# Gated attention in a two-layer block: backward direction in backward token order, GpSimd copying queries, keys and finished blocks

## The reference, cut to what matters

```
bcum = cumsum(a, within the chunk)
inter = (q * exp(bcum)) @ s
decay[t, s] = exp(bcum[t] - bcum[s])        for s <= t, per key column
scores[t, s] = sum_k q[t, k] k[s, k] decay[t, s, k]
intra = scores @ v
s_new = s * exp(total) + (k * exp(total - bcum)).T @ v
```

## Time and profile before

| | us |
|---|---|
| median of 3 runs | 3181.17 (3180.76 to 3181.77) |
| the profiled execution | 3191.26 |
| its span, first to last instruction | 3189.5 |
| PE busy in the span | 2585.3 (81%) |
| DVE busy | 1668.5 (52%) |
| ACT busy | 913.6 (29%) |
| POOL busy | 848.5 (27%) |

### The profile page before, as it was taken

One profiled execution on the slowest core, in us unless ns is written; L12 is line 12 of the kernel. 1 busy time (PEld: TensorE's weight loads), 2 busy tenths in 40 slices (PEclk: granted clock), 3 DMA queues, 4 the chain that ended last, 5 costly groups with the idle time before them and its releaser, 6 DMA issues. The chain is left out here.

```text
span 3189.5 us, 47594 instructions
## 1 busy us (share of the span) xinstructions
PE 2585.3 (81%) x19846; PEld 2207.7 (69%) x19846; DVE 1668.5 (52%) x2456; ACT 913.6 (29%) x1438; POOL 848.5 (27%) x779
## 2 busy tenths in 40 slices
PE   4899999965788763555594899999679999998787
PEld 1577677755677752554473677878579999998665
DVE  2136887542346524787556546465555554554333
ACT  1114233311132223355311323232233334332211
POOL 0211111126466531555322211111012211121321
PEclk7899999987789876777797899999889999999898
DMA  6613545533324312010243223333332222210521
GB/s 255 214 51 93 160 134 161 161 125 81 84 78 120 101 42 74 17 42 25 86 140 90 80 99 113 103 109 106 123 112 69 92 74 87 74 54 1 205 99 60
DMA packets 290100, 318.04 MB, mean 100 GB/s; under 512 B 109663, under 2 KB 235046, under 8 KB 287198
## 3 DMA queue, kind: packets, MB, share of 16 engines
q1 hardware_dynamic: 288816, 311.62, 30.8%
q10 hardware_dynamic: 1070, 3.37, 0.3%
HBM read 202.30 MB, written 112.56 MB: 99 GB/s over the span
## 5 line engine op out<-in xcount | busy, mean ns | idle before, releaser
L2668 PE MATMUL PS<-Q,K 128*128 128x128 f32 x2560 | 296.0, 277 | 33.0 <-DMA K<-k_d 24.1
L2668 PEld LDWEIGHTS PS<-Q,K 128*128 128x128 f32 x2560 | 292.5, 194 | 35.5 <-issue 28.1
L2789 POOL TENSOR_TENSOR weights_lo<-weights,weights_hi 128x1664 fp32r<-128x1664 f32 x32 | 121.4, 3793 | 566.6 <-ACT weights_hi L2747 566.6
L2695 PE MATMUL PS<-V_hi,weights_hi 128*128 128x258 f32 x832 | 239.1, 287 | 5.3 <-DVE H L2898 2.7
L376 PE MATMUL PS<-hT_hi,w_in_hi 128*128 128x512 f32 (+1 forms) x640 | 239.7, 375 | 0.0
L377 PE MATMUL PS<-hT_lo,w_in_hi 128*128 128x512 f32 (+1 forms) x640 | 236.4, 369 | 0.0
L378 PE MATMUL PS<-hT_hi,w_in_lo 128*128 128x512 f32 (+1 forms) x640 | 236.2, 369 | 0.0
L2696 PE MATMUL PS<-V_lo,weights_hi 128*128 128x258 f32 x832 | 236.1, 284 | 0.0
L2697 PE MATMUL PS<-V_hi,weights_lo 128*128 128x258 f32 x832 | 235.2, 283 | 0.0
L376 PE MATMUL PS<-h_hi,w_in_hi 128*128 128x512 f32 (+1 forms) x624 | 228.3, 366 | 5.1 <-PEq L109 5.1
L2169 PE MATMUL PS<-w_out_hi,y_in_hi 128*128 128x512 f32 x416 | 168.8, 406 | 73.1 <-DVE y_in_lo L2107 39.7
(11 more groups left out here) (378 smaller groups left out, 5941.6 us busy)
## 6 DMA issues: line engine op xcount, KB each, us to landing
chunk_in<-in_d SPq DMA_DIRECT2D x40, 512.0 KB, 3.4
w_in<-in_e_w_in_dram SPq DMA_DIRECT2D x30, 512.0 KB, 5.0
xnew<-in_o_w_in_dram SPq DMA_DIRECT2D x30, 512.0 KB, 6.1
in_d<-xnat SPq DMA_DIRECT2D x20, 640.0 KB, 6.1
modw<-in_mod_w_dram SPq DMA_DIRECT2D x8, 1536.0 KB, 19.1
xnat<-in_mod_w_dram SPq DMA_DIRECT2D x8, 1536.0 KB, 7.5
v_d<-xnew SPq DMA_DIRECT2D x16, 640.0 KB, 2.9
k_d<-xc SPq DMA_DIRECT2D x16, 640.0 KB, 2.9
```

Source lines behind the costliest of these rows:

```text
L2668: last = pe.matmul(PS[:, 4 + x % 4, (j - j0) * P:(j - j0 + 1) * P], K[:, kt, j * P:(j + 1) * P], Q[:, kt, i * P:(i + 1) * P], start=(kt == ...
L2695: pe.matmul(out, wh, VH[:, j, q], start=(j == seen[0]), stop=False)
```

## The change

The backward rows are now held in backward token order (context and latent part each reversed), so that in both directions an earlier token is the key and a later one the query. What then follows:

- The left half of each block holds keys and the right half queries in one tensor `X`; DVE forms both (`operands`), distances keep one sign, and ACT's absolute value and POOL's clearing and key product go. All DVE operations of a level come in two halves of 640 elements.
- Levels run from 64 down to 1. Level 64 (`far`) and 32 (`near`) are rectangles, which ACT copies from PSUM to `AT`. The five fine levels form blocks of 32x32 by 80 small matmuls each, with one masked copy of 128x640 into `BL`; POOL copies the finished blocks into `AT` (`blocks`, 8 copies a head).
- Queries and keys are loaded once in token order (`nat`), and POOL copies them reversed (`backward`, 4 copies a head). The low-rank gate input is reversed once by DVE (`lgr`), and PE turns the values with a reversed identity (`flip`, ACT evicts them).
- Forward and backward states advance together, 9 steps on 128 rows. The readout has 4 matmuls a chunk in place of 2. Decayed keys and queries move from POOL to DVE. `AT` and `qd` get a second half for the backward direction and are cleared once by POOL.
- The masks are narrower, and the constants loaded for the stage fewer.

```diff
-LEVELS = [1, 2, 4, 8, 16, 32, 64]
+LEVELS = [64, 32, 16, 8, 4, 2, 1]
+FINE = [16, 8, 4, 2, 1]
...
+    for b in FINE:
+        c[f"parted{b}"] = np.tile(lr(b)[:32, :32], (4, 1))
+    c["diag32"] = (2 * ((p % 32) == np.arange(32)[None])).astype(one)
+    c["flip"] = np.eye(P, dtype=one)[::-1].copy()
...
+                def load_nat(h):
+                    for d in range(2):
+                        sp.dma_start(nat[rows(d), 0], A.gq_d[h // 2][rows(h % 2)]).then_inc(s["nat_in"], 16)
+                    sp.dma_start(nat[rows(1), 1], A.gk_d[h // 2][rows(h % 2)]).then_inc(s["nat_in"], 16)
...
+                    for c in range(NCH):
+                        for r in range(4):
+                            t = slice(c * CH + 32 * r, c * CH + 32 * r + 32)
+                            last = pe.matmul(PS[in_block(r), prep_bank(1), 32 * c:32 * c + 32], k[rows(0), h % 2, t], q[rows(0), h % 2, t],
+                                             start=True, stop=True)
+                    last.then_inc(s["base_ps"], 1)
...
+                        for i, n in enumerate(chunks(j)):
+                            last = pe.matmul(PS[:, prep_bank(j), i * P:(i + 1) * P], G.c("flip"), V[:, h % 2, at(1, n)], start=True, stop=True)
+                        last.then_inc(s["vr_ps"], 1)
...
+                def far(n):
+                    for c in range(NCH):
+                        for d in range(2):
+                            out = PS[0:64, far_bank(d, c), 64 * (c % 8):64 * (c % 8) + 64]
+                            last = pe.matmul(out, X[rows(d), n % 2, c * CH:c * CH + 64], X[rows(d), n % 2, c * CH + 64:c * CH + CH], start=True, stop=True)
+                    last.then_inc(s["scored"], 1)
...
+                def near(n):
+                    for c in range(NCH):
+                        for u in range(2):
+                            for d in range(2):
+                                t = c * CH + 64 * u
+                                last = pe.matmul(PS[in_block(2 * u), d, 32 * c:32 * c + 32], X[rows(d), n % 2, t:t + 32], X[rows(d), n % 2, t + 32:t + 64],
+                                                 start=True, stop=True)
+                    last.then_inc(s["scored"], 1)
...
+                    h, lv = n // NLEV, n % NLEV
+                    pe.wait_ge(s["x_ok"], n + 1)
+                    if lv == 2:
+                        pe.wait_ge(s["near_sb"], h + 1)
+                    else:
+                        pe.wait_ge(s["merged"], fine(n))
+                    for c in range(NCH):
+                        for r in range(4):
+                            for d in range(2):
+                                t = slice(c * CH + 32 * r, c * CH + 32 * r + 32)
+                                last = pe.matmul(PS[in_block(r), d, 32 * c:32 * c + 32], X[rows(d), n % 2, t], X[rows(d), n % 2, t], start=True, stop=True)
+                    last.then_inc(s["scored"], 1)
...
+                def readout(h):
+                    if h == 0:
+                        pe.wait_ge(s["zero"], 4)
+                        pe.wait_ge(s["s_zero"], 1)
+                    pe.wait_ge(s["chain"], (NCH - 1) * (h + 1))
+                    pe.wait_ge(s["far_sb"], h + 1)
+                    pe.wait_ge(s["near_sb"], h + 1)
+                    pe.wait_ge(s["blk_sb"], 8 * (h + 1))
                     for c in range(NCH):
-                        last = pe.matmul(col(c), KN[:, c], V[:, h % 2, c], start=True, stop=True)
-                    last.then_inc(s["outer"], 1)
-
-                def readout(h):
-                    for d in range(2):
-                        pe.wait_ge(chain[d], (NCH - 1) * (h + 1))
-                    pe.wait_ge(s["merged"], 3 * NLEV * (h + 1))
-                    for c in range(NCH):
-                        pe.matmul(col(c), V[:, h % 2, c], AT[:, h % 2, c], start=True, stop=False)
-                        last = pe.matmul(col(c), S[:, c], qd[:, h % 2, c * CH:c * CH + CH], start=False, stop=True)
+                        n = ORDER[1].index(c)
+                        t = slice(c * CH, c * CH + CH)
+                        pe.matmul(col(c), V[:, h % 2, c], AT[:, h % 2, 0, c], start=True, stop=False)
+                        pe.matmul(col(c), VR[:, n], AT[:, h % 2, 1, n], start=False, stop=False)
+                        pe.matmul(col(c), S[:, c], qd[:, h % 2, 0, t], start=False, stop=False)
+                        last = pe.matmul(col(c), S[:, n], qd[:, h % 2, 1, t], start=False, stop=True)
                     last.then_inc(s["o_ps"], 1)
...
+                        (far, near, scores)[min(lv, 2)](n)
                         if h == 0 and lv == 1:
                             turn(0)
-                        if lv == 0 and h:
-                            readout(h - 1)
-                        if lv == 1 and h + 1 < GLA_HEADS:
-                            gates(h + 1)
-                        if lv == 2:
+                        if lv == 1:
+                            if h + 1 < GLA_HEADS:
+                                gates(h + 1)
+                            if h:
+                                readout(h - 1)
+                        if lv == 3:
                             if h:
                                 variance(h - 1)
                             if h + 1 < GLA_HEADS:
                                 base(h + 1)
                         if lv == 4:
+                            flip(h)
+                        if lv == 5:
                             outer(h)
                         if lv == 6 and h + 1 < GLA_HEADS:
                             turn(h + 1)
...
-                    act.activation(e, e, ACT.Abs).then_inc(s["away"], 1)
-                    act.wait_ge(s["away"], n + 1)
-                    act.activation(e, e, ACT.Exp, scale=-1.0 / 16).then_inc(s["expd"], 1)
+                    act.wait_ge(s["dist"], 2 * n + 2)
+                    act.activation(e, e, ACT.Exp, scale=1.0 / 16).then_inc(s["expd"], 1)
...
+                def far(h):
+                    act.wait_ge(s["scored"], NLEV * h + 1)
+                    if h == 0:
+                        act.wait_ge(s["zero"], 2)
+                    if h >= 2:
+                        act.wait_ge(s["o_ps"], h - 1)
+                    for d in range(2):
+                        v = placed(h, d, slice(0, 64), slice(64, 128))
+                        act.activation(v[:, 0:8], PS[0:64, d, :].rearrange("p (c t) -> p c t", t=64), ACT.Copy)
+                        last = act.activation(v[:, 8:NCH], PS[0:64, far_bank(d, 8), 0:128].rearrange("p (c t) -> p c t", t=64), ACT.Copy)
+                    last.then_inc(s["far_sb"], 1)
+
+                def near(h):
+                    act.wait_ge(s["scored"], NLEV * h + 2)
+                    for d in range(2):
+                        for u in range(2):
+                            last = act.activation(placed(h, d, in_block(2 * u), in_block(2 * u + 1)),
+                                                  PS[in_block(2 * u), d, 0:32 * NCH].rearrange("p (c t) -> p c t", t=32), ACT.Copy)
+                    last.then_inc(s["near_sb"], 1)
...
-                    pool.tensor_tensor(KL[:, n % 2], E[:, n % 3], k[:, h % 2], ALU.mult).then_inc(s["k_ok"], 1)
...
+                def backward(h):
+                    for j, dst in enumerate((q, k)):
+                        for i, (lo, hi) in enumerate(TURNED):
+                            if h or j or i:
+                                pool.wait_ge(s["turned"], 4 * h + 2 * j + i)
+                            pool.tensor_copy(dst[rows(1), h % 2, lo:hi], nat[rows(1), j, lo:hi][:, ::-1]).then_inc(s["turned"], 1)
+
...
+                def blocks(h):
+                    pool.wait_ge(s["merged"], NF * (h + 1))
+                    pool.wait_ge(s["turned"], 4 * min(h + 2, GLA_HEADS))
+                    if h >= 2:
+                        pool.wait_ge(s["o_ps"], h - 1)
                     for d in range(2):
-                        last = pool.memset(half(QL[:, n % 2], LEVELS[n % NLEV], d, d == 1), 0.0)
-                    last.then_inc(s["q_zero"], 1)
-
-                def keys(n):
-                    h = n // NLEV
-                    pool.wait_ge(s["expd"], n + 1)
-                    if n % NLEV == 0:
-                        pool.wait_ge(qk_in[h % 2], 64 * (h // 2 + 1))
-                    if n:
-                        pool.wait_ge(s["q_zero"], n)
-                    if n >= 1 and done(n):
-                        pool.wait_ge(s["qd_ok"], done(n))
-                    if n >= 2:
-                        pool.wait_ge(s["scored"], 3 * (n - 1))
-                    pool.tensor_tensor(KL[:, n % 2], E[:, n % 3], k[:, h % 2], ALU.mult).then_inc(s["k_ok"], 1)
-
-                def decayed(h):
-                    pool.wait_ge(qk_in[h % 2], 64 * (h // 2 + 1))
-                    pool.wait_ge(s["kd_ex"], h + 1)
-                    if h:
-                        pool.wait_ge(s["k_ok"], NLEV * (h - 1) + 7)
-                    else:
```

(70 more changed lines are left out.)

286 lines of the change are left out of this document (167 added, 119 removed).

## The result

The changed kernel takes 3127.83 us (median of 4 runs, 3122.36 to 3131.05), the kernel before 3181.47 beside it: 0.9825 of its time [0.9806, 0.9845]. That is 1.7% shorter, well outside the scatter. The forecast was 3126. In the profiled execution the span is 3120.5 us.

A forecast was written before the change was run, and what follows sets the result against it. No engine was full; each level was taken as a chain DVE, POOL, PE, DVE. The stage's terms, 28 + 53 + 61 + 61 + 46 + 29.8 = 278.8 us against 333.9, gave 3136 profiled and 3126 timed, range 3098 to 3176.

The forecast's parts named there:

- log wait: DVE's wait for ACT's logarithm of the gates, put at 7 us a head, 8 before the change.
- a new wait of 6 for the base: DVE's diagonal waits for the next head's base matmuls, queued on PE behind readout, scores and variance: 6 us, new.
- Collisions: DVE made to wait by POOL's 12 copies a head: about 3 us a head, range 0 to 9.
- Eight block copies: POOL's copies of 320 elements each head: 0.65 us each, 5.2 us in all, range 3.4 to 5.8.
- tail: From the last merge to the end: block copies 5.2, readout 11.3, from eviction on 13.3, together 29.8 us.
- three signs of being wrong: A level's scores over 6 us, half-width DVE operations over 1 us, or waits for POOL's block copies in middle heads.
- a level's 160 records: PE's 80 fine score matmuls of 64x32 in a level: 3.2 us, between 1.1 and 8.4 by overlap.
- The rival in which PE becomes the bound: Small matmuls share nothing, 105 ns each, so PE needs 78 us a head: 3211 us, chance 0.08.
- the rival at 3104: Cover holds better: column groups overlap, base early, clock high, 5 to 6 us less a head; chance 0.18.
- heads 1 and 2: Middle heads of the stage: DVE's work plus its waits, 61 us each against 72.5 before.
- head 3: Last head, preparing no other: DVE 33.5, state steps 1.4 and waits 11, 46 us to its last merge.
- the 44.6 + 3: A middle head on DVE: 44.6 us of its own operations plus 3 us of collisions with POOL.

The follow-up runs named there:

- e3: Changed kernel with the next head's base matmuls on PE right behind its gates, ahead of the readout: 3111.87 us, 0.9759 of the kernel before.
- e6: Changed kernel with 40 fine score matmuls of 64 columns a level in place of 80 of 32, timing only: 3113.33 us, 0.9767 of the kernel before.
- e1: Kernel before the change without POOL's clearing of the queries and the waits for it: 3172.26 us, 0.9947 of the kernel before.
- e2: Changed kernel with each of the 80 fine score matmuls of a level issued twice: 3214.01 us, 1.0083 of the kernel before.
- e5: Changed kernel with 72 of the 80 fine score matmuls of a level streaming 64 columns instead of 32: 3128.23 us, 0.9810 of the kernel before.
- e8: e7 with, in the last head, first fine scores ahead of head 2's readout, variance and eviction a level later: 3118.27 us, 0.9776 of the kernel before.
- e10: e8 with DVE's gate sum and scan of the next head one level later: 3124.67 us, 0.9798 of the kernel before.
- e12: e7 with DVE's gate sum and scan a level later and the ACT and PE queues reordered to match: 3109.36 us, 0.9762 of the kernel before.
- e7: e3 with the last head's readout split, its 40 records that need no block copy first: 3109.50 us, 0.9746 of the kernel before.

## Why the prediction was right

**The stage's chain.** The view that DVE's own order of work and waits sets the stage after the change held: it forecast 7 us of log wait a head (measured 7.14 and 7.15, and 11.66 in head 0) and a new wait of 6 for the base (4.79, 5.26, 5.90), and e3, which takes only the second away, gained 12.6 of the 17.8 us that it costs; 5.3 went over to waits for scores. What the view lacked is the supply of PE's instructions: e6 takes 11 to 15 us away with DVE's order unchanged. That the removed link through POOL was part of the gain is shown by e1; by itself it is not the whole.

**DVE.** Predicted 0.82 us a half and measured 0.81 to 0.83 undisturbed, at all levels, so the finest levels' steps cost nothing. The merges took 0.87 for 0.88, clearing and diagonal 0.8 for 0.8, the state steps 346 ns. But the sum of durations was too long, since operations that follow each other overlap in the records; in head 2, with no wait between them:

```profile
1402.13 0.82 DVE L2103 TENSOR_TENSOR lev_e<-gla_b 128x640 f32<-128x640 f32 x1
1402.87 0.82 DVE L2104 TENSOR_TENSOR lev_e<-gla_b 128x640 f32<-128x640 f32 x1
1403.60 0.82 DVE L2114 TENSOR_TENSOR lev_x<-lev_e,gla_k 128x640 f32<-128x640 f32 x1
```

They start 0.735 us apart, 0.085 less than they last; for 28 halves that is 2.4 us a head. Collisions were put at 3 us a head: the 112 halves have 97.6 us where 0.82 each would be 91.8, so 5.8 in all, 1.9 in each of three heads.

**POOL.** Eight block copies were put at 5.2 us and took 4.01 in the tail, 0.45 each and 0.51 from start to start, where 0.65 was taken; 44.4 us busy against "under 50". They made no wait in the middle heads, and of the three signs of being wrong only one was touched: 19 of the 112 halves took over 1 us, all beside POOL.

**The scores, mis-sized twice.** The prediction put a level's 160 records at 3.2 us, assuming that row groups overlap and column groups partly. A burst takes 1.56 at a granted clock of 1.00 and 1.87 at 0.50, so row and column groups all overlap: (1.56 - 0.21, the length of one record) / 160 is 8.4 ns a record. But bursts often stand in the middle for 1 to 3 us, and e2, e5 and e6 show that this comes with the number of instructions. The two errors cancel, which is luck: a burst with one gap is 3 to 4 us. The rival in which PE becomes the bound needed 90 ns a matmul; 20 were measured. What half of those instructions costs is 11 to 15 us (e6), half of the way to the rival at 3104 or more.

**Heads.** Start 26.6 us for 28, head 0 53.3 for 53, heads 1 and 2 56.5 and 57.1 for 61, head 3 48.9 for 46, tail 28.4 for 29.8. In the middle heads the waits were as charged (stretches of 56 and 58 us less the 43.3 and 44.5 that DVE is busy: 12.7 and 13.5, for 13.5), and the work was 3 to 4 us less than the 44.6 + 3, by the overlap above and the smaller collisions. Head 3 has DVE busy for 32.8 us (34.9 forecast) and idle for 16.2 (11 forecast): I charged the readout of head 2 and little behind it, but then DVE waits again for scores that PE can't deliver, and e8 shows PE setting the length of that head. In the tail three small errors nearly cancel: from the last merge to the readout 4.2 us for 5.2, the readout 12.1 for 11.3, and from the eviction on 12.1 for 13.3. Of that last piece 1.1 us are the variance, 2.42 us in this execution and 3.55 in the one before.

**Profile and median.** The stage was predicted at 278.8 and measured at 270.8; the span outside it also fell by 5.8 us in that one execution (3.7 before the stage, 2.1 behind). So the profiled execution was 14 us faster than the 3136 I forecast for it, while its median missed by 2. The profiled execution before lay 10 above its median and that after 5 below its own. The forecast's error of 14 us for the profiled execution and the 15 by which that offset changed cancel almost exactly, so the agreement to 2 us is luck. The stage's error of 8 us, 13% of what the stage gave back, is the honest size.

## What to carry to other kernels

Count PE's instructions, not only its columns: 160 records of 64x32 run in 1.6 us, but a stream of them was delivered at 28 ns each, and the gaps show as "issue" in the middle of a group with no releaser. Count the packets of the instruction queue in the stage: they are PE's records, weight loads with them, by 256. Before moving an operation to cover a wait, ask what the wait itself covers: the readout lay under the logarithm's wait, and reordering around it in one queue (e10) or all three (e12) exchanged one wait for another, while moving the 2 us base ahead of an 11 us readout (e3) was worth 12.6 us. When a tail has a copy in front of a summed product, start the sum with the terms that don't need the copy (e7).

## What the runs showed of the hardware

- At a granted clock of 1.00, PE records of 64x32 on two row groups and four column groups start 8.4 ns apart; 80 records on one row group and four column groups (L1767) took 0.96 us, 9.4 ns apart.
- Doubling the columns of 3200 records cost 0.1 us in the stage; doubling the records cost 88. In long streams PE ran 128 matmul records and stood for 2.0 to 2.2 us. The queue named instruction had one packet for 256 PE instructions (8, 24, 37 and 62 packets for 7.6, 24.0, 36.5 and 61.5), and in 43 of 43 gaps over 1 us (e2 and the changed kernel) PE went on 1.2 to 1.6 us after such a packet had ended. What sets when a packet is sent was not tried.
- Copies on POOL and half-width operations of DVE that lay beside each other took turns: 1.06 and 0.93 us each, both 0.99 us from start to start, where they take 0.82 and 0.45 alone.
- Behind the same 2.63 us of idle PE, the same six matmuls took 2.42 us at a granted clock of 1.00, 3.36 at 0.70 and 4.11 at 0.62. The first two are one program in two executions, so what a kernel did before does not settle it by itself; what does was not tried.
